# SSD decays in a hybrid decoder step: one VectorE minimum per chunk, one ScalarE exponential with a bias per head

## What is computed

```python
seg = acs[..., :, None] - acs[..., None, :]           # token i less token j
decay = jnp.exp(jnp.where(tri, seg, -jnp.inf))         # only j <= i
wts = cb[:, :, :, None] * decay * dt_t[..., None, :]   # cb = C . B of the group
y_diag = jnp.einsum('ncgeij,ncjgep->ncigep', wts, xc)
decay_end = jnp.exp(acs[..., -1:] - acs) * dt_t        # the last i of a chunk
states = jnp.einsum('ncjgs,ncgej,ncjgep->ncgeps', bc, decay_end, xc)
```

## Time and profile before

| | us |
|---|---|
| Median of 3 runs (range) | 1359.13 (1357.59 to 1359.99) |
| The profiled execution's own time | 1357.39 |
| Its span, first to last instruction | 1355.5 |
| PE busy | 1302.3 (96%) |
| DVE busy | 800.2 (59%) |
| ACT busy | 631.5 (47%) |
| POOL busy | 486.1 (36%) |

### The profile page before, as it was taken

One profiled execution on the slowest core, in us unless ns is written; L12 is line 12 of the kernel. 1 busy time (PEld: TensorE's weight loads), 2 busy tenths in 40 slices (PEclk: granted clock), 3 DMA queues, 4 the chain that ended last, 5 costly groups with the idle time before them and its releaser, 6 DMA issues. The chain is left out here.

```text
span 1355.5 us, 29049 instructions
## 1 busy us (share of the span) xinstructions
PE 1302.3 (96%) x11346; PEld 1249.2 (92%) x11346; DVE 800.2 (59%) x1570; ACT 631.5 (47%) x1412; POOL 486.1 (36%) x414
## 2 busy tenths in 40 slices
PE   5999999999999999999999999899998999999997
PEld 5999999999999999999998999798997988979997
DVE  4445354553555533745445256577979879697464
ACT  4333332443433433333344364467577665765352
POOL 1545432555333553334542232003335343252031
PEclk9999999999999999999999999999998999999999
DMA  6574433754425633448532174333553635653351
GB/s 193 147 212 124 105 97 102 200 143 107 110 80 173 190 98 84 125 124 260 131 102 75 47 241 110 116 95 111 148 175 114 191 110 150 201 155 107 92 175 66
DMA packets 313543, 182.48 MB, mean 135 GB/s; under 512 B 75248, under 2 KB 302272, under 8 KB 313024
## 3 DMA queue, kind: packets, MB, share of 16 engines
q1 hardware_dynamic: 313408, 180.64, 46.6%
HBM read 155.01 MB, written 46.41 MB: 149 GB/s over the span
## 5 line engine op out<-in xcount | busy, mean ns | idle before, releaser
L1878 POOL TENSOR_TENSOR wlo<-w,whi 128x1024 fp32r<-128x1024 f32 x95 | 228.3, 2404 | 421.1 <-ACT whi L1518 421.1
L1355 PE MATMUL at_proj<-uhi,whi 128*128 128x272 f32 x1536 | 333.7, 298 | 1.9 <-PEq L145 1.3
L1355 PE MATMUL at_proj<-uhi,wlo 128*128 128x272 f32 x1536 | 317.8, 288 | 0.0
L1355 PE MATMUL at_proj<-ulo,whi 128*128 128x272 f32 x1536 | 317.5, 288 | 0.0
L1518 ACT ACTIVATE whi<-w 128x1024 fp32r<-128x1024 f32 x95 | 100.7, 1060 | 331.5 <-PE at_proj L1355 302.7
L1355 PEld LDWEIGHTS at_proj<-uhi,whi 128*128 128x128 f32 x1536 | 239.3, 189 | 5.2 <-issue 2.2
L1355 PEld LDWEIGHTS at_proj<-ulo,whi 128*128 128x128 f32 x1536 | 241.7, 189 | 0.0
L1355 PEld LDWEIGHTS at_proj<-uhi,wlo 128*128 128x128 f32 x1536 | 240.6, 189 | 0.0
L2363 PE MATMUL kept<-uhi,whi 128*128 128x272 f32 (+1 forms) x744 | 164.2, 301 | 2.7 <-DVE wlo L2763 1.9
L2363 PE MATMUL kept<-uhi,wlo 128*128 128x272 f32 (+1 forms) x744 | 156.3, 291 | 0.0
L2363 PE MATMUL kept<-ulo,whi 128*128 128x272 f32 (+1 forms) x744 | 155.9, 290 | 0.0
(11 more groups left out here) (378 smaller groups left out, 2402.1 us busy)
## 6 DMA issues: line engine op xcount, KB each, us to landing
w<-in_attn_w_in_dram SPq DMA_DIRECT2D x88, 512.0 KB, 4.3
w<-in_ssd_w_in_dram SPq DMA_DIRECT2D x38, 512.0 KB, 4.2
sd_h<-in_state_ssm_dram SPq DMA_DIRECT2D x16, 512.0 KB, 6.5
sd_bc<-acs_p SPq DMA_DIRECT2D x16, 512.0 KB, 5.3
out_s_ssm_dram<-sd_h SPq DMA_DIRECT2D x16, 512.0 KB, 3.5
w<-in_ssd_w_out_dram SPq DMA_DIRECT2D x13, 512.0 KB, 3.7
at_k_cache<-in_cache_kv_w_dram SPq DMA_DIRECT2D x384, 16.0 KB, 2.8
at_v_cache<-in_cache_kv_w_dram SPq DMA_DIRECT2D x24, 256.0 KB, 4.1
```

What stands on the lines that cost most here:

```text
L1355: last = pe.matmul(proj[:, r, h, 0:HALF], a[:, r, kk * P:(kk + 1) * P], b[:, kk, h * HALF:(h + 1) * HALF], start=(kk == 0 and a is whi and ...
L1878: pool.tensor_tensor(wlo[:, r], w[:, r], whi[:, r].bitcast(F32), ALU.subtract).then_inc(wlo_ready, 1)
```

## The change

DVE's eight `tensor_scalar` of a prompt chunk become one `tensor_tensor` that takes the minimum of `bc` and the chunk's own `acs`, spread along the inner dimension. ACT then adds `acs_bias` = log dt - acs as the bias of an exponential per head, eight of 128x128. `to_end` is no exponential of its own any more but a copy of the finished `decay`'s last column, so it comes behind them, and WT waits for it as well, since it overwrites `decay`. The sample's chunk keeps its eight DVE instructions, with minimum and addition instead of subtraction and minimum. The setup step AC writes to the new buffer `acs_bias`.

```diff
@@ ACT, chunk_decays
-                act.activation(to_end[:, n % 2, :], decay[:, n % 2, :, P - 1], ACT.Exp).then_inc(te_ready, 1)
-                act.wait_ge(te_ready, 4 * e + k)
-                x = decay[:, n % 2].rearrange("p h i -> p (h i)")
-                act.activation(x, x, ACT.Exp).then_inc(decay_ready, 1)
+                for h in range(HG):
+                    at = HG * e + h
+                    x = decay[:, n % 2, h, :]
+                    last = act.activation(x, x, ACT.Exp, bias=acs_bias[:, c, at:at + 1])
+                last.then_inc(decay_ready, 1)
+                act.wait_ge(decay_ready, n + 1)
+                act.activation(to_end[:, n % 2, :], decay[:, n % 2, :, P - 1], ACT.Copy).then_inc(te_ready, 1)
@@ DVE, AC
-                    dve.tensor_tensor(acs[:, 0:LAST, :], acs[:, 0:LAST, :], dt_log[:, 0:LAST, :], ALU.subtract)
+                    dve.tensor_tensor(acs_bias[:, 0:LAST, :], dt_log[:, 0:LAST, :], acs[:, 0:LAST, :], ALU.subtract)
...
@@ DVE, SG
-                    for h in range(HG):
-                        at = HG * e + h
-                        if k == 0:
+                    if k == 0:
+                        for h in range(HG):
+                            at = HG * e + h
                             b = bc[0:NS, n % 2].rearrange("p h i -> p (h i)")[:, h * NS:(h + 1) * NS]
-                        else:
-                            b = bc[:, n % 2, h, :]
-                        last = dve.tensor_scalar(decay[0:r, n % 2, h, 0:r], b, acs[0:r, c, at:at + 1],
-                                                 dt_log[0:r, c, at:at + 1], ALU.subtract, ALU.min)
+                            last = dve.tensor_scalar(decay[0:r, n % 2, h, 0:r], b, acs[0:r, c, at:at + 1],
+                                                     acs_bias[0:r, c, at:at + 1], ALU.min, ALU.add)
+                    else:
+                        own_acs = acs[:, c, HG * e:HG * (e + 1)].unsqueeze(2).broadcast_to([P, HG, P])
+                        last = dve.tensor_tensor(decay[:, n % 2], bc[:, n % 2], own_acs, ALU.min)
@@ DVE, WT
                     dve.wait_ge(decay_ready, n + 1)
+                    if k:
+                        dve.wait_ge(te_ready, 4 * e + k)
```

More of the change, by code:

```diff
@@ L2094, in ssd_phase @@
         acs = m.sb("acs", [P, TT, NHEADS])
+        acs_bias = m.sb("acs_bias", [P, TT, NHEADS])
         par = m.sb("par", [P, 2, XBC, PAR])
@@ L2800, in _ @@
                     dve.wait_ge(acs_ready, 1)
-                    dve.tensor_tensor(acs[:, 0:LAST, :], acs[:, 0:LAST, :], dt_log[:, 0:LAST, :], ALU.subtract)
-                    dve.tensor_tensor(acs[0:NS, LAST, :], acs[0:NS, LAST, :], dt_log[0:NS, LAST, :], ALU.subtract) \
+                    dve.tensor_tensor(acs_bias[:, 0:LAST, :], dt_log[:, 0:LAST, :], acs[:, 0:LAST, :], ALU.subtract)
+                    dve.tensor_tensor(acs_bias[0:NS, LAST, :], dt_log[0:NS, LAST, :], acs[0:NS, LAST, :], ALU.subtract) \
                         .then_inc(shifted, 1)
```

## The result

The changed kernel takes 1360.53 us in the median of 16 runs (1357.75 to 1362.39), the kernel before 1358.86 in as many (1353.44 to 1359.99). The ratio is 1.0019, 95% interval 1.0010 to 1.0027: slower by about 2.6 us, clear of noise and small.

The account below looks back on a forecast made before the run. TensorE, busy 96% of the span, was taken to bound the kernel. Stalls of 8.31 less 6.24 returned (+2.07) and clock +0.5 on 1357.39 gave 1359.9, or 1361.6 us as median; range 1354.5 to 1367.

Parts of the forecast that it names:

- VectorE's part: Per prompt chunk, one merged minimum takes 1.37 us, 1.7 us less than the eight instructions; 27 us off VectorE's busy time.
- ScalarE's part: Per prompt chunk, eight exponentials and a copy replace two exponentials: +1.26 us on ACT, 20 us in all.
- Where it meets TensorE: ACT's lateness delays copies that empty TensorE's banks, mostly the tail rows': 8.31 us of stalls in five places.
- What VectorE gives back: VectorE's relief in chunks 4, with TensorE coming later, removes 6.24 us of stalls, leaving +2.07 net.
- Waits behind the new order: Waits of WT, POOL and SP's loads behind the later exponentials and to_end add nothing to the sum.
- The clock: The low-clock stretch behind the stall at 1043 goes, -1.65 us; 1.3 new stretches come, +2.1; net +0.5.
- A: Slower: each held bank copy is followed by a stretch at the lower clock; +7.0 us, 1366.1; chance 0.12.
- B: Slower: the exponentials don't overlap, 2.14 us per chunk; +9.3, 1368.4; a dear inner broadcast, +8.3, is alike; chance 0.08.
- C: Faster: ACT's lateness stays off TensorE; stalls of 9.49 us and two clock stretches go; -12.8, 1346; chance 0.17.
- The sum: Profiled execution 1357.39 plus stalls 2.07 plus clock 0.5 makes 1359.9; the median stands 1.74 higher, so 1361.6 us.

Follow-up runs that it names:

- the tail rows early: Changed kernel with the tail rows' product and copy moved before HT 4: 1359.82 us, ratio 1.0017; the same move in the kernel before: 0.9997.
- VectorE's part alone: Changed kernel with the merged minimum kept, but one 128x1024 exponential per prompt chunk and no head bias: 1348.1 us, ratio 0.9928 to the kernel before.
- the pair: Kernel before with two wide VectorE instructions per prompt chunk, minimum then bias addition, and one exponential on ScalarE: 1354.5 us, ratio 0.9987.

## Why the prediction was right, point by point

- *VectorE's part.* Right: 1.31 us in the mean for 1.37; busy time -27.3 for -27.
- *ScalarE's part.* Slightly small: +1.38 per chunk for +1.26. Eight took 2.45 and not 2.34: the overlap of two neighbours is 0.09 us ((8 x 0.389 - 2.45) / 7) and not the 0.11 that I read from two copies. The Trainium skill's figure ("ScalarE: Activation LUTs", section What ACT_TABLE_LOAD costs), 0.093, was the better one, and the 1.38 that followed from it is what the trace has.
- *Where it meets TensorE.* Right in size, and in place but for one item: a part of the lateness stalls TensorE just ahead, at `x_rows`, so that HN 2 waits 1.17 and not 1.4 to 2.4 us. HT 1: 0.73 for 0.67. Group 0: 0.67 + 1.17 less the old 0.33 is 1.51 for 1.42; group 2 the same; group 1: 0.44 + 1.09 + 2.36 less the old 1.44 is 2.45 for 2.43; group 3: 2.23 for 2.37. In sum 8.4 for 8.31. The decays of group 1's chunk 2 weren't "long ready" for ScalarE: before, VectorE finished them at 1016.27, 0.03 us before `to_end`; since the minimum is shorter now, the sum doesn't suffer. The run with the tail rows early shows what was incomplete: the copy is the first wait that this lateness meets, not the only one.
- *What VectorE gives back.* The sum is about right (6.4 for 6.24), its parts aren't. The 2.00 and the 1.19 went. The 1.08 at 1113, which I said stays, went: `tmp` comes 2.85 us later than before, behind ScalarE's `z`, and TensorE later still, by the stalls ahead of it and a stretch at the lower clock there (below). Of 2.15, 0.81 stays (0.73 foreseen). Of the 1.03 and 0.34 that I said go, 0.63 and 0.34 stay. What went against the forecast (1.23 us with a stall of 0.15 that it hadn't) and what stayed against it (1.05) nearly cancel: that the sum fits this well is luck.
- *Waits behind the new order.* VectorE sits idle 1.02 to 1.03 us before WT 2 in groups 0 to 2 of the changed kernel, until `to_end`, 0.24 us behind the exponentials, is there, and 0.50 in group 3; in group 1 that is why 1.09 of the old 1.44 stays ahead of OS, as the working had it. "None adds to the sum" left out POOL's chain from `raw` to YA, which decides in group 0 once the tail rows are out of the way, and POOL's addition before chunk 4's `tmp`, which takes 3.26 us for 2.14 and holds `tmp` for 1.27.
- *The clock.* The stretch behind 1043 went, and a new one came in group 2, at the stall at HN 2; net 0 in the scan for +0.5. Windows of the changed kernel (us, busy of the engines, PEclk, DMA, GB/s):

```profile
1030.00:1035.00 5.00, 4.00 (x19) 3.91 (x20) 4.18 (x7) 2.95 (x5) 2.84 (x2) 0.66 0.51 135
1110.00:1115.00 5.00, 3.83 (x24) 3.59 (x24) 1.66 (x3) 4.88 (x11) 3.32 (x3) 0.83 0.13 31
```

- *The rivals.* A (more clock stretches) did not come: two of the scan's stalls have one behind them, as before. B (no overlap) is excluded by the 2.45 us, its other form (a dear inner broadcast) by the 1.31. C (the relief is collected) is what the run with VectorE's part alone measures, -9.8 for my -12.8; it needed ScalarE's part left out. Both stretches went there (3.4 us), but the stalls fell by 5.6 us and not 9.49: 1.10 of the 2.00 stays, and 0.97 names the tail rows.
- *The sum.* +2.5 against the median before, for +2.6. The prediction's own addition is 0.1 us short (1357.39 + 2.07 + 0.5 + 1.74 = 1361.7).

The span of the profiled execution grew by 3.2 us, more than the 2.0 of idle time. The rest came before the changed code: TensorE's item at 869.24 before stands at 870.25, with one more stretch at the lower clock ahead of it, at 864. Whether that is chance can't be told from one execution each, so of the profiled growth of 3.2 us the working explains 2.0.

## What to carry to other kernels

Moving work off a busy engine pays by the waits that name it, and costs where the work lands; here the same trade gained 4.3 us in chunk 4 and lost 7.3 us in chunks 2 and 3, so it is to be made place by place. Before an instruction is added to a queue, look for the copy next behind it that empties a PSUM bank, and compare the copy's end with the start of the item that reuses the bank: a gap of 0.05 us without a stall in the profile is a wait not yet seen. And when that copy is moved away, follow the late engine's other consumers too, through third engines in order. What a merged instruction saves is to be checked on the engine beside it as well: here POOL's addition grew by 1.1 us.

## What the runs showed of the hardware

An exponential of 128x128 with a bias per partition takes 0.389 us and eight in a row 2.45, where one of 128x1024 takes 1.06: splitting by head costs 1.39 us. A minimum of 128x1024 with an operand spread along the inner dimension takes 1.21 to 1.23 us in 12 of 16 places, as much as the subtraction of that shape between full operands (`wlo`, 1.22). In chunk 4 of group 1, beside POOL's addition of 128x512, the minimum takes 1.22 us and POOL 3.25; eight instructions of 128x128 in its place take 3.86 for 2.13 undisturbed, and POOL 2.14. VectorE isn't spared always: the second wide instruction of the pair takes 2.19 there.

A stall's length alone doesn't tell whether a stretch at 1.2 GHz follows. In the two main kernels one began 0.4 to 2.0 us behind stalls of 1.44 and 2.00 (before) and of 2.36 and, in group 2, 1.17 (changed). None began behind 2.15 (before) or behind 1.17 and 1.18 in groups 0 and 3 (changed). With the tail rows early the stall of 2.15 in the kernel before did have one behind it, and so did that of 1.94 in group 0 of the changed kernel.
